# Sums of squares of the attention heads: one fp32 product with ones, or two fp32r products with ones over high and low halves

## The chip, the cores and the metric

The kernel is one program on one core of a Trainium2 chip. The metric is the time of one execution on the device in microseconds (us). Three runs of the kernel before are at hand, and one more execution was recorded by the hardware profiler.

## What is computed

Two transformer blocks over 512 tokens of width 1024. The first has two layers: a forgetting attention with 12 heads, then a retention with 12 heads, each beside 4 heads of attention over 256 memory tokens. The second block joins a long convolution with a gated linear attention (GLA) of 4 heads and a feed-forward layer. The change touches the norm of each head, in retention and in GLA:

```python
out = out.transpose(1, 0, 3, 2, 4).reshape(B, S, H, dv)      # 12 retention heads, dv = 128
out = out * lax.rsqrt(jnp.mean(out * out, axis=-1, keepdims=True) + EPS)
```

The GLA heads, also 128 wide, are normed in the same way, with a gain. All is in float32.

## The kernel before

Activations lie with features on the 128 partitions and the 512 tokens along the free dimension. A sum over the features of a head is therefore a sum over partitions, and the kernel makes it on TensorE: a product of a 128x128 matrix of ones with the squares puts the sum into every partition of a PSUM bank.

Projections are made with split operands. Each float32 operand is written as a high half in fp32r (wh, HH, OH, YH) and a low half that is the operand less its high half (wl, HL, OL, YL); a product is then three fp32r products, high by high, high by low and low by high. The copy that makes a high half runs on ACT (`copy`). Low halves of weights are made on DVE at first and on POOL (GpSimd) later, those of activations by one or the other in turn. The weights come as 294 tiles of 128x1024 by DMA on the SP queue, in a fixed plan; `split_next` makes their halves and `take` hands out the next one. `unit_f` and `unit_t` are a projection of 256 columns in two halves, 24 products of 512 columns (or 48 of 256) each; `beside` is a function that is called between the halves.

The order of the work is written out by hand. Each engine has a list (`Line`) to which the build functions append, and each engine runs its list strictly in the order of the calls. An instruction waits for the marks in its `after`.

The retention loop runs over pairs of heads, p = 0 to 5. Its calls around the change, in the kernel before and in the changed one:

```python
unit_f(HH, HL, beside=(lambda: even_norm(p - 1)) if p else None)
if p:
    ret_attend(2 * p - 1)
    keep_q()
...
rotate(p)
if p:
    ret_square(2 * p - 1)
unit_t(HH, HL, beside=(lambda: ret_rstd(2 * p - 1)) if p else None)
```

`ret_attend` puts the output of a head into bank 5 or 7. `ret_square` squares it on ACT into SQ. `ret_rstd` makes the product of ones with SQ in bank 6, and ACT makes R = exp(-0.5 ln(mean + eps)) from it, with two loads of function tables. `ret_norm` multiplies by the gate and splits the result into OH and OL, the operands of the output projection. `rotate(p)` is the rotary embedding of the next pair: SP copies QX and KX with partitions swapped, by eight small DMAs (QS, KSw), and DVE multiplies by COS and SIN and adds, ending with QR and then KR, which the scores read. The squares of an even head are called at the end of an iteration, and their product between the halves of the next one's first projection. Heads 10 and 11 are finished between the first steps of the output projection.

In GLA, `gla_square` squares a head into a temporary tile (T1 or T2; in the profile both are T), and `gla_rstd` makes the products for a pair of heads, i = 0 and then i = 1. `scales` makes row norms of the inputs with the same matrix of ones, the first time at 29 us. In the profile all instructions have line 77, that of the function that replays the lists, so that groups are told apart by their tiles.

Of the kernel before, what the change touches and what calls it, by code (L numbers as in the profile page):

```python
# [8 lines left out]
ALU = mybir.AluOpType  # L9
ACT = mybir.ActivationFunctionType  # L10
AX = mybir.AxisListType
F32 = mybir.dt.float32
F32R = mybir.dt.float32r
# [6 lines left out]
T = 512  # L20
# [157 lines left out]
def build(nc, a, out, stack):  # L178
    V, S, G, PE, SP = nc.vector, nc.scalar, nc.gpsimd, nc.tensor, nc.sync
# [7 lines left out]
    def at(name, shape, kb, dt=F32, extra=0):  # L187
        return nc.alloc_sbuf_tensor_at(name, shape, dt, offset=BASE + int(kb * KB) + extra)

    pe, dve, act, pool, sp = (Line(count("s_" + n)) for n in ("pe", "dve", "act", "pool", "sp"))  # L190
# [5 lines left out]
    s_c = [count("s_c%d" % i) for i in range(10)]  # L196
# [11 lines left out]
    OH = at("OH", [128, 16, T], 92, F32R)  # L208
    OL = at("OL", [128, 16, T], 124, F32R)
    km = [at("km0", [128, 4, 256], 108), at("km1", [128, 4, 256], 156)]  # L210
    vm = [at("vm0", [128, 2, T], 112), at("vm1", [128, 2, T], 160)]
    ident = at("ident", [128, 128], 164)
    ones = at("ones", [128, 128], 164.5)
    identb = at("identb", [128, 128], 165, BF16)
    maskb = at("maskb", [128, 128], 165.25, BF16)
    par = at("par", [128, NPAR], 165.5)
# [7 lines left out]
    eps, mod, modc = small["eps"], small["mod"], small["modc"]  # L224
# [6 lines left out]
    def copy(dst, src, after=()):  # L231
        return act.do(S.activation, dst, src, ACT.Copy, after=after)
# [4 lines left out]
    def afn(dst, src, f, after=(), **k):  # L237
        return act.do(S.activation, dst, src, f, after=after, **k)

    def tt(dst, x, y, op, after=()):  # L240
        return dve.do(V.tensor_tensor, dst, x, y, op, after=after)
# [9 lines left out]
    def vcopy(dst, src, after=()):  # L251
        return dve.do(V.tensor_copy, dst, src, after=after)

    def mm(dst, w, x, start, stop, after=(), mark=False):
        f = pe.do if mark else pe.quiet
        return f(PE.matmul, dst, w, x, start=start, stop=stop, skip_group_check=True, after=after)
# [5 lines left out]
    bank = [Bank(psum[:, i, :]) for i in range(8)]  # L262
# [199 lines left out]
    R = at("R", [128, T], C0 + 38)  # L462
# [3 lines left out]
    M = {}  # L466
    tfree = [[], []]
# [7 lines left out]
    def add_square(t, n, first, after, acc=None, scale=1.0, name="acc"):  # L475

        acc = acc or ACC
        i, q, tf = temp()
        m = afn(q[:, 0:n], t, ACT.Square, after=[*after, *tf], scale=scale)
        if first:  # L480
            m = vcopy(acc[:, 0:n], q[:, 0:n], after=[m, *M.get(name + " free", [])])
        else:
            m = tt(acc[:, 0:n], acc[:, 0:n], q[:, 0:n], ALU.add, after=[m, M[name]])
        tfree[i] = [m]
        M[name] = m
# [6 lines left out]
    def rstd(src, after, n, dim, dst, dst_free, b):  # L492

        last = M.pop("last", None)
        e = mm(b.ap[:, 0:n], ones[:, :], src, True, last is None, after=[*after, *b.free, M["cst"]], mark=True)
        if last:
            i, q, m = last
            e = mm(b.ap[:, 0:n], ones[:, :], q[:, 0:n], False, True, after=[m], mark=True)
            tfree[i] = [e]
        m = afn(dst, b.ap[:, 0:n], ACT.Ln, after=[e, M["eps"], *dst_free], scale=1.0 / dim, bias=eps[:, 0:1])  # L500
        b.free = [m]
        return e, afn(dst, dst, ACT.Exp, after=[m], scale=-0.5)
# [41 lines left out]
    for _ in range(2):  # L544
        load_raw()
    m_cst = sp.dma(SP.dma_start, ident[:, :], a["cst"][:, 0:128], s_c[0])
    m_cst = sp.dma(SP.dma_start, ones[:, :], a["cst"][:, 128:256], s_c[0])
    m_cst = sp.dma(SP.dma_start, maskf[:, :], a["cst"][:, 256:384], s_c[0])
    M["cst"], M["par"] = m_cst, m_par
    m_mem = [sp.dma(SP.dma_start, MX[:, 4 * i:4 * i + 4, :], a["memT"][:, 4 * i:4 * i + 4, :], s_mem[i])  # L550
# [3 lines left out]
    m = dve.do(V.memset, eps[:, 0:1], 1e-6)  # L554
# [13 lines left out]
    q, m, w = take_128()  # L568
# [6 lines left out]
    unit_f(HH, HL)  # L575
    for k in range(8):
        add_square(MX[:, k, :], 256, k == 0, [m_mem[k // 4]], ACC2, name="accm")
    rcol = small["tq"]

    def scales(acc, name, n, dst, c, b, b2, free=()):  # L580

        e = mm(b.ap[:, 0:n], ones[:, :], acc[:, 0:n], True, True, after=[M[name], m_cst, *b.free], mark=True)
        w = n // 128
        for t in range(w):
            e2 = mm(b2.ap[:, t:t + 1], acc[:, 128 * t:128 * t + 128], ones[:, 0:1], t == 0, t == w - 1,
                    after=[*b2.free], mark=(t == w - 1))
        M[name + " free"] = [e2]
        m = afn(dst, b.ap[:, 0:n], ACT.Ln, after=[e, M["eps"], *free], scale=1.0 / 1024, bias=eps[:, 0:1])
        m2 = afn(rcol[:, c:c + w], b2.ap[:, 0:w], ACT.Ln, after=[e2], scale=1.0 / 1024, bias=eps[:, 0:1])
        b.free, b2.free = [m], [m2]  # L590
        return afn(dst, dst, ACT.Exp, after=[m], scale=-0.5), afn(rcol[:, c:c + w], rcol[:, c:c + w], ACT.Exp, after=[m2], scale=-0.5)
# [202 lines left out]
    m = tt(CT[:, :], bank[4].ap, R[:, :], ALU.mult, after=[f_done, M["rx"]])  # L794
    bank[4].free = [m]
    m = afn(CB[:, :], CT[:, :], ACT.Abs, after=[m], bias=P("bf"))
    m2 = ts(CT[:, :], CT[:, :], P("bf"), 0.0, ALU.add, ALU.min, after=[m])
    m = afn(CB[:, :], CB[:, :], ACT.Exp, after=[m], scale=-1.0)
# [9 lines left out]
    m = afn(CB[:, :], CB[:, :], ACT.Ln, after=[m], bias=one)  # L808
    for j in range(2):
# [4 lines left out]
    m = tt(CB[:, :], CT[:, :], CB[:, :], ALU.subtract, after=[m, m2])  # L814
    m = dve.do(V.tensor_tensor_scan, CT[:, :], ones[:, 0:1].to_broadcast([128, T]), CB[:, :], 0.0, ALU.mult, ALU.add,
               after=[m])
# [23 lines left out]
    for i in range(4):  # L840
        e = tr(bank[6].ap[:, 128 * i:128 * i + 128], CT[:, 128 * i:128 * i + 128],
               after=[M["ct"], *bank[6].free], mark=(i == 3))
# [116 lines left out]
    SQ = at("SQ", [128, T], C0 + 28)  # L959
# [111 lines left out]
        M["pt readers", h % 2] = M["pt readers"] = [e]  # L1071

    def ret_square(h):
        b = bank[(5, 7)[h % 2]]
        M["sq"] = afn(SQ[:, :], b.ap, ACT.Square, after=[M["o", h], *M.get("sq free", [M["pe"]])])

    def ret_rstd(h):
        e, M["rn"] = rstd(SQ[:, :], [M["sq"]], T, 128, R[:, :], M["R free"], bank[6])
        M["sq free"] = [e]

    def ret_norm(h):
        m = M["rn"]
# [145 lines left out]
    banks = [bank[2:6], [bank[6], bank[7], bank[0], bank[1]]]  # L1228
# [4 lines left out]
    i, t, tf = temp()  # L1233
    m = tt(t[:, :], R[:, :], R[:, :], ALU.mult, after=[rm, *tf])
    m = tt(t[:, :], bank[7].ap, t[:, :], ALU.mult, after=[m, e2])
    bank[7].free, tfree[i] = [m], [m]
    R2 = at("R2", [128, T], C0 + 20)
    m = afn(R2[:, :], t[:, :], ACT.Ln, after=[m], scale=1.0 / 1024, bias=eps[:, 0:1])
    tfree[i] = [m]
    m = afn(R2[:, :], R2[:, :], ACT.Exp, after=[m], scale=-0.5)  # L1240
# [8 lines left out]
    for k in range(2):  # L1249
        e = mm(bank[4].ap[0:1, :], FT[:, k, 1, 0:1], UR[:, k, :], k == 0, k == 1, after=[*bank[4].free], mark=(k == 1))  # L1250
# [28 lines left out]
    for half in range(2):  # L1279
        o = 2 - 2 * half  # L1280
# [7 lines left out]
        for j in range(2):  # L1288
            c = 2 * half + j
            i, t, tf = temp()  # L1290
            m = conv(j, 8 + c, t[:, :], tf)
            m = tt(UT[:, c, :], t[:, :], X1[:, j, :], ALU.mult, after=[m, x1[j], en_read])
# [58 lines left out]
    banks = [[bank[6], bank[7], bank[2], bank[3]], [bank[4], bank[5], bank[6], bank[7]]]  # L1351
# [10 lines left out]
    YH, YL = at("YH", [128, 8, T], 92, F32R), at("YL", [128, 8, T], 108, F32R)  # L1362
    inverse = []
    for c in range(4):
        b = bank[4 + c]
        for odd in range(2):
            for cs in range(2):
                for ft in range(2):
                    last = odd == 1 and cs == 1 and ft == 1
                    e = mm(b.ap[:, 256 * odd:256 * odd + 256], Y[:, 4 * ft + 2 * cs + odd, 128 * c:128 * c + 128],  # L1370
                           IT[:, ft, cs, 256 * odd:256 * odd + 256], odd + cs + ft == 0, last,
                           after=[M["y", ft, 2 * cs + odd], m_it, *b.free], mark=last)
# [49 lines left out]
    q, m, w = take_128()  # L1422
# [187 lines left out]
        M["o", 0] = M["o", 1] = e  # L1610
        ss_free[:] = [e]

    def gla_square(h):
        it, t, tf = temp()
        M["gsq", h] = it, t, afn(t[:, :], bank[4 + h].ap, ACT.Square, after=[M["o", h], *tf])

    def gla_rstd(banks):
        for h in range(2):
            it, t, m = M["gsq", h]
            M["gr", h] = mm(banks[h].ap, ones[:, :], t[:, :], True, True, after=[m, *banks[h].free], mark=True)  # L1620
            tfree[it] = [M["gr", h]]
        for h in range(2):
            m = afn(RH[h][:, :], banks[h].ap, ACT.Ln, after=[M["gr", h], *rh_free[h]], scale=1.0 / 128, bias=eps[:, 0:1])
            banks[h].free = [m]
        for h in range(2):
            M["gr", h] = afn(RH[h][:, :], RH[h][:, :], ACT.Exp, after=[m], scale=-0.5)
# [23 lines left out]
    def out2(n, kh, hooks=None):  # L1650
        features(YH, YL, range(4 * kh, 4 * kh + 4), T, kh == 0, kh == 1, y_h, OUT_BANKS[n], hooks=hooks)
# [60 lines left out]
    for h in range(2):  # L1712
        for d in range(2):
            gla_within(0, d, h, False, d == 1)
        gla_square(h)
    gla_scores(1, 0, bank[0:2])
    for d in range(2):
        gla_ends(1, d)
    gla_context(1)
    gla_rstd(bank[2:4])  # L1720

    def start_second():
        gla_start(1)
# [18 lines left out]
        gla_within(1, d, h, d == 0, False)  # L1742
    gla_across(1, False)
    for h in range(2):
        gla_square(h)
    out2(1, 0, [lambda: None, lambda: gla_rstd(bank[2:4]), lambda: None, lambda: None])
    out2(2, 0)
    gla_norm(1, 0)
    gla_low(1, 0)
# [195 lines left out]
```

How the kernel before makes its waits and increments, by code:

```python
    def replay(self, eng):  # L72
        for w in self.work:
            if w[0] is None:
                eng.wait_ge(w[1], w[2])
            else:
                i = w[0](*w[1], **w[2])
                if w[3] is not None:
                    i.then_inc(w[3], w[4])
```

## Time and profile before

| | |
|---|---|
| runs | 1677.83 us median of 3 (1674.85 to 1679.32) |
| profiled execution, its own time | 1679.68 us |
| its span, first to last instruction | 1677.9 us |
| PE (TensorE) busy | 1632.9 us, 97% |
| DVE (VectorE) busy | 777.7 us, 46% |
| ACT (ScalarE) busy | 646.1 us, 39% |
| POOL (GpSimd) busy | 509.2 us, 30% |
| mean granted clock of TensorE | 0.991 of full speed |

PE is busy almost all the time. Matmuls are pipelined, so their durations overlap; the distance between the starts of two of them tells what one costs. A granted clock of 1.00 is 2.4 GHz, one of 0.50 is 1.2 GHz. An idle time in square brackets behind a row is that of its engine just before, with what ended it.

### The profile page before, as it was taken

What the parts mean: (1) busy time and instruction counts of PE and PEld (TensorE: products, weight loads), DVE (VectorE), ACT (ScalarE), POOL (GpSimd) and SP (SyncE); (2) the same over time, 40 slices, a digit from 0 to 9 for tenths busy, and PEclk for the clock granted to TensorE, in tenths of its full rate; (3) what the DMA queues carried; (4) which work ended last, traced back from release to release, by engine and by line L of the source; (5) the groups of instructions that cost most, each with busy time, mean ns of one, the idle gap of its engine ahead of it and who ended that gap; (6) DMA issues with size and microseconds to landing.
All of it is one profiled execution on the core that took longest, in us unless ns stands there. A gap on an engine that the chain in (4) does not pass through costs nothing.

```text
span 1677.9 us, 19891 instructions
## 1 busy us (share of the span) xinstructions
PE 1632.9 (97%) x8222; PEld 1333.7 (79%) x8222; DVE 777.7 (46%) x1183; ACT 646.1 (39%) x966; POOL 509.2 (30%) x245
## 2 busy tenths in 40 slices
PE   8999999999999999999999999989999899999997
PEld 7888888888878778888887767678878688888885
DVE  7877665656565344333333654752253411111113
ACT  8532333333233333444444463234434443232322
POOL 0000000000044434333333415443223355554541
PEclk9999999999999999999999999999999899999999
DMA  6454424343435223333332222122102123222321
GB/s 242 154 175 132 151 94 139 102 144 101 144 128 199 101 88 101 101 101 101 101 105 88 84 92 98 48 79 70 49 26 73 66 101 101 89 100 90 104 83 50
DMA packets 52385, 175.98 MB, mean 105 GB/s; under 512 B 6332, under 2 KB 6972, under 8 KB 51912
## 3 DMA queue, kind: packets, MB, share of 16 engines
q1 hardware_dynamic: 52296, 174.73, 30.9%
q8 instruction: 64, 1.05, 0.3%
q14 instruction: 25, 0.20, 0.0%
HBM read 169.44 MB, written 2.12 MB: 102 GB/s over the span
## 4 chain that ended last, share of the span: by engine, by line
PE 86%; DVE 8%; ACT 3%; issue 1%; POOL 1%; DMA 1%; DVEq 0%; ACTq 0%; SPq 0%
PE banks L77 86%; DVE T L77 1%; DVE TM L77 1%; ACT L77 1%; DVE ada L77 1%; DVE X L77 1%; DVE wl L77 1%; POOL wl L77 0%; DVE HL L77 0%; DVE Sc L77 0%; ACT R L77 0%; DVE Y L77 0%; ACT wh L77 0%; ACT T L77 0%; ACT Sc L77 0%
## 5 line engine op out<-in xcount | busy, mean ns | idle before, releaser
L77 POOL TENSOR_TENSOR wl<-raw,wh 128x1024 fp32r<-128x1024 f32 x173 | 426.7, 2471 | 531.5 <-ACT wh L77 531.4
L77 PE MATMUL banks<-HH,wh 128*128 128x512 f32 x1040 | 417.6, 402 | 11.7 <-ACT HH L77 11.4
L77 PE MATMUL banks<-HL,wh 128*128 128x512 f32 x1040 | 406.4, 393 | 0.8 <-DVE HL L77 0.7
L77 ACT ACTIVATE wh<-raw 128x1024 fp32r<-128x1024 f32 x246 | 258.1, 1054 | 342.5 <-PE banks L77 339.3
L77 PE MATMUL banks<-HH,wl 128*128 128x512 f32 x1040 | 286.8, 392 | 2.9 <-POOL wl L77 2.9
L77 PEld LDWEIGHTS banks<-HH,wh 128*128 128x128 f32 x1040 | 197.0, 189 | 59.4 <-ACT HH L77 13.0
L77 PEld LDWEIGHTS banks<-HL,wh 128*128 128x128 f32 x1040 | 196.9, 189 | 46.0 <-DVE HL L77 4.0
L77 PEld LDWEIGHTS banks<-HH,wl 128*128 128x128 f32 x1040 | 196.4, 189 | 45.7 <-POOL wl L77 3.7
L77 POOL TENSOR_TENSOR OL<-T,OH 128x512 fp32r<-128x512 f32 x21 | 28.1, 1340 | 505.2 <-ACT OH L77 505.2
L77 PE MATMUL banks<-wh,HH 128*128 128x256 f32 x448 | 130.5, 291 | 0.0
L77 PE MATMUL banks<-wl,HH 128*128 128x256 f32 x448 | 126.7, 283 | 0.0
L77 PE MATMUL banks<-wh,HL 128*128 128x256 f32 x448 | 126.7, 283 | 0.0
L77 DVE TENSOR_TENSOR wl<-raw,wh 128x1024 fp32r<-128x1024 f32 x73 | 87.7, 1221 | 53.1 <-ACT wh L77 52.9
L77 PE MATMUL banks<-OH,wh 128*128 128x512 f32 x256 | 103.8, 405 | 1.9 <-DVE Zt L77 1.7
L77 PE MATMUL banks<-OL,wh 128*128 128x512 f32 x256 | 99.8, 390 | 0.0
L77 PE MATMUL banks<-FHI,wh 128*128 128x512 f32 x256 | 99.6, 389 | 0.0
L77 PE MATMUL banks<-FLO,wh 128*128 128x512 f32 x256 | 99.6, 389 | 0.0
L77 DVE SCALAR_TENSOR_TENSOR X<-banks,mod,X 128x512 f32<-128x512 f32 x40 | 30.0, 751 | 147.7 <-PE banks L77 147.6
L77 PEld LDWEIGHTS banks<-wh,HH 128*128 128x128 f32 x448 | 85.9, 192 | 2.0 <-issue 1.4
L77 PEld LDWEIGHTS banks<-wh,HL 128*128 128x128 f32 x448 | 85.9, 192 | 1.5 <-issue 1.4
L77 DVE TENSOR_TENSOR T<-T 128x512 f32<-128x512 f32 x32 | 24.6, 769 | 133.2 <-ACT T L77 133.2
L77 PEld LDWEIGHTS banks<-wl,HH 128*128 128x128 f32 x448 | 85.8, 192 | 0.0
(291 smaller groups left out, 2439.2 us busy)
## 6 DMA issues: line engine op xcount, KB each, us to landing
raw<-wst_dram SPq DMA_DIRECT2D x294, 512.0 KB, 3.3
CB<-sums_dram SPq DMA_DIRECT2D x12, 256.0 KB, 3.1
D<-dec_dram SPq DMA_DIRECT2D x12, 256.0 KB, 2.8
X<-xT_dram SPq DMA_DIRECT2D x4, 512.0 KB, 5.9
out_dram<-X SPq DMA_DIRECT2D x8, 256.0 KB
QS<-QX SPq DMA_DIRECT2D x24, 64.0 KB, 2.5
KSw<-KX SPq DMA_DIRECT2D x24, 64.0 KB, 2.0
MX<-memT_dram SPq DMA_DIRECT2D x2, 512.0 KB, 9.2
```

The costliest lines, as they stand in the source:

```text
L77: i = w[0](*w[1], **w[2])
```

## The change

The matrix of ones is now an fp32r tile, `onesr`, and `ones` is the same memory read as float32. The DMA brings the values to `onesf`, and DVE casts them into `onesr` behind the squares of the memory.

`ret_square` still squares into SQ on ACT; then ACT copies SQ into OH[h], which is free until the head's result is written there, and DVE puts SQ less that into OL[h]. `ret_rstd` makes two fp32r products in one accumulation, ones by OH[h] and ones by OL[h], in place of the float32 product of ones with SQ. In GLA, `gla_square` and `gla_rstd` do the same with YH and YL. There are 12 + 4 such heads. The other products with ones stay float32.

```diff
--- before.py
+++ after.py
@@ -210,7 +210,8 @@
     km = [at("km0", [128, 4, 256], 108), at("km1", [128, 4, 256], 156)]
     vm = [at("vm0", [128, 2, T], 112), at("vm1", [128, 2, T], 160)]
     ident = at("ident", [128, 128], 164)
-    ones = at("ones", [128, 128], 164.5)
+    onesr = at("ones", [128, 128], 164.5, F32R)
+    ones = onesr[:, :].bitcast(F32)
     identb = at("identb", [128, 128], 165, BF16)
     maskb = at("maskb", [128, 128], 165.25, BF16)
     par = at("par", [128, NPAR], 165.5)
@@ -544,7 +545,8 @@
     for _ in range(2):
         load_raw()
     m_cst = sp.dma(SP.dma_start, ident[:, :], a["cst"][:, 0:128], s_c[0])
-    m_cst = sp.dma(SP.dma_start, ones[:, :], a["cst"][:, 128:256], s_c[0])
+    onesf = at("onesf", [128, 128], 184)
+    m_cst = sp.dma(SP.dma_start, onesf[:, :], a["cst"][:, 128:256], s_c[0])
     m_cst = sp.dma(SP.dma_start, maskf[:, :], a["cst"][:, 256:384], s_c[0])
     M["cst"], M["par"] = m_cst, m_par
     m_mem = [sp.dma(SP.dma_start, MX[:, 4 * i:4 * i + 4, :], a["memT"][:, 4 * i:4 * i + 4, :], s_mem[i])
@@ -575,11 +577,12 @@
     unit_f(HH, HL)
     for k in range(8):
         add_square(MX[:, k, :], 256, k == 0, [m_mem[k // 4]], ACC2, name="accm")
+    M["ones"] = vcopy(onesr[:, :], onesf[:, :], after=[m_cst])
     rcol = small["tq"]
 
     def scales(acc, name, n, dst, c, b, b2, free=()):
 
-        e = mm(b.ap[:, 0:n], ones[:, :], acc[:, 0:n], True, True, after=[M[name], m_cst, *b.free], mark=True)
+        e = mm(b.ap[:, 0:n], ones[:, :], acc[:, 0:n], True, True, after=[M[name], M["ones"], *b.free], mark=True)
         w = n // 128
         for t in range(w):
             e2 = mm(b2.ap[:, t:t + 1], acc[:, 128 * t:128 * t + 128], ones[:, 0:1], t == 0, t == w - 1,
@@ -1071,12 +1074,20 @@
         M["pt readers", h % 2] = M["pt readers"] = [e]
 
     def ret_square(h):
+
         b = bank[(5, 7)[h % 2]]
-        M["sq"] = afn(SQ[:, :], b.ap, ACT.Square, after=[M["o", h], *M.get("sq free", [M["pe"]])])
+        m = afn(SQ[:, :], b.ap, ACT.Square, after=[M["o", h], *M.get("sq free", [M["pe"]])])
+        mh = copy(OH[:, h, :], SQ[:, :], after=[m])
+        ml = tt(OL[:, h, :], SQ[:, :], OH[:, h, :].bitcast(F32), ALU.subtract, after=[mh, m])
+        M["sq free"] = M["sq"] = [ml]
 
     def ret_rstd(h):
-        e, M["rn"] = rstd(SQ[:, :], [M["sq"]], T, 128, R[:, :], M["R free"], bank[6])
-        M["sq free"] = [e]
+        b = bank[6]
+        mm(b.ap, onesr[:, :], OH[:, h, :], True, False, after=[*M["sq"], *b.free])
+        e = mm(b.ap, onesr[:, :], OL[:, h, :], False, True, mark=True)
+        m = afn(R[:, :], b.ap, ACT.Ln, after=[e, *M["R free"]], scale=1.0 / 128, bias=eps[:, 0:1])
+        b.free = [m]
+        M["rn"] = afn(R[:, :], R[:, :], ACT.Exp, after=[m], scale=-0.5)
 
     def ret_norm(h):
         m = M["rn"]
@@ -1610,15 +1621,20 @@
         M["o", 0] = M["o", 1] = e
         ss_free[:] = [e]
 
-    def gla_square(h):
+    def gla_square(i, h):
+
         it, t, tf = temp()
-        M["gsq", h] = it, t, afn(t[:, :], bank[4 + h].ap, ACT.Square, after=[M["o", h], *tf])
-
-    def gla_rstd(banks):
+        k = 4 + 2 * i + h
+        m = afn(t[:, :], bank[4 + h].ap, ACT.Square, after=[M["o", h], *tf])
+        mh = copy(YH[:, k, :], t[:, :], after=[m])
+        M["gsq", h] = tt(YL[:, k, :], t[:, :], YH[:, k, :].bitcast(F32), ALU.subtract, after=[mh, m])
+        tfree[it] = [M["gsq", h]]
+
+    def gla_rstd(i, banks):
         for h in range(2):
-            it, t, m = M["gsq", h]
-            M["gr", h] = mm(banks[h].ap, ones[:, :], t[:, :], True, True, after=[m, *banks[h].free], mark=True)
-            tfree[it] = [M["gr", h]]
+            k = 4 + 2 * i + h
+            mm(banks[h].ap, onesr[:, :], YH[:, k, :], True, False, after=[M["gsq", h], *banks[h].free])
+            M["gr", h] = mm(banks[h].ap, onesr[:, :], YL[:, k, :], False, True, mark=True)
         for h in range(2):
             m = afn(RH[h][:, :], banks[h].ap, ACT.Ln, after=[M["gr", h], *rh_free[h]], scale=1.0 / 128, bias=eps[:, 0:1])
             banks[h].free = [m]
@@ -1712,12 +1728,12 @@
     for h in range(2):
         for d in range(2):
             gla_within(0, d, h, False, d == 1)
-        gla_square(h)
+        gla_square(0, h)
     gla_scores(1, 0, bank[0:2])
     for d in range(2):
         gla_ends(1, d)
     gla_context(1)
-    gla_rstd(bank[2:4])
+    gla_rstd(0, bank[2:4])
 
     def start_second():
         gla_start(1)
@@ -1742,8 +1758,8 @@
         gla_within(1, d, h, d == 0, False)
     gla_across(1, False)
     for h in range(2):
-        gla_square(h)
-    out2(1, 0, [lambda: None, lambda: gla_rstd(bank[2:4]), lambda: None, lambda: None])
+        gla_square(1, h)
+    out2(1, 0, [lambda: None, lambda: gla_rstd(1, bank[2:4]), lambda: None, lambda: None])
     out2(2, 0)
     gla_norm(1, 0)
     gla_low(1, 0)
```

DVE, the rotation of the pair p = 1, before (QS and KSw are the swapped copies, PT and PTodd the score tiles):

```order
L77 TENSOR_TENSOR T_85<-QX,COS 128x512
L77 TENSOR_TENSOR QS<-QS,SIN 128x512
L77 TENSOR_TENSOR QR<-T_85,QS 128x512
L77 TENSOR_TENSOR T_86<-KX,COS 128x512
L77 TENSOR_TENSOR KSw<-KSw,SIN 128x512
L77 TENSOR_TENSOR KR<-T_86,KSw 128x512
L77 TENSOR_TENSOR PT<-banks,D_111 128x512
```

and after:

```order
L77 TENSOR_TENSOR T_85<-QX,COS 128x512
L77 TENSOR_TENSOR QS<-QS,SIN 128x512
L77 TENSOR_TENSOR QR<-T_85,QS 128x512
L77 TENSOR_TENSOR T_86<-KX,COS 128x512
L77 TENSOR_TENSOR KSw<-KSw,SIN 128x512
L77 TENSOR_TENSOR KR<-T_86,KSw 128x512
L77 TENSOR_TENSOR OL<-SQ,OH 128x512
L77 TENSOR_TENSOR PT<-banks,D_112 128x512
```

The subtraction for head 1 stands between KR and the first product of the scores.

PE, between the two halves of the value projection of p = 1:

```order
 L77 MATMUL banks<-wh,HL 128x256
 L77 MATMUL banks<-wl,HH 128x256
-L77 MATMUL banks<-SQ,ones 128x512
+L77 MATMUL banks<-OH,ones 128x512
+L77 MATMUL banks<-OL,ones 128x512
 L77 MATMUL banks<-wh,HH 128x256
 L77 MATMUL banks<-wh,HL 128x256
```

Two products take the place of one, between the same neighbours; the first of them now waits for DVE.

ACT, in the second pair of GLA heads:

```order
 L77 ACTIVATE YH<-T_86 128x512
 L77 ACTIVATE T_85<-banks 128x512
-L77 ACTIVATE T_86<-banks 128x512
+L77 ACTIVATE YH<-T_85 128x512
+L77 ACTIVATE T_86<-banks 128x512
+L77 ACTIVATE YH<-T_86 128x512
 L77 ACTIVATE wh<-raw 128x1024
 L77 ACT_TABLE_LOAD
```

Two copies stand ahead of the weight copy and of the table load for R.

## Rows read from the trace of the kernel before

**Rows 1.** The page, chain that ended last, share of the span by engine
```profile
PE 86%; DVE 8%; ACT 3%; issue 1%; POOL 1%; DMA 1%; DVEq 0%; ACTq 0%; SPq 0%
```

**Rows 2.** PE's waits between 660 and 900 us: us in total, times, longest
```profile
PE banks L77 <- DVE OL L77: 0.2, 1, 0.2
```

**Rows 3.** Timeline of PE: start us, us, engine line op out<-in xcount
```profile
687.71 1.02 PE L77 MATMUL banks<-SQ,ones 128*128 128x512 f32 x2
...
891.72 1.07 PE L77 MATMUL banks<-OH,wl 128*128 128x512 f32 x4
892.63 1.02 PE L77 MATMUL banks<-SQ,ones 128*128 128x512 f32 x2
893.72 0.40 PE L77 MATMUL banks<-OL,wh 128*128 128x512 f32 x1
```

**Rows 4.** Timeline of ACT and DVE beside it; ACT's group of copies
```profile
682.15 0.60 ACT L77 ACTIVATE SQ<-banks 128x512 f32<-128x512 f32 x1 [1.46 <-PE banks L77]
...
687.58 0.69 DVE L77 TENSOR_TENSOR QS<-QS,SIN 128x512 f32<-128x512 f32 x1 [4.38 <-DMA QS<-QX]
691.16 0.69 DVE L77 TENSOR_TENSOR KR<-T,KSw 128x512 f32<-128x512 f32 x1
...
L77 ACT ACTIVATE OH<-T 128x512 fp32r<-128x512 f32 x32 | 20.2, 631 | 117.1 <-DVE T L77 117.1
```

**Rows 5.** Timelines of PE and DVE, heads 3, 5, 7, 9: the product, then KR
```profile
729.85 1.02 PE L77 MATMUL banks<-SQ,ones 128*128 128x512 f32 x2
733.63 0.69 DVE L77 TENSOR_TENSOR KR<-T,KSw 128x512 f32<-128x512 f32 x1
...
771.98 1.02 PE L77 MATMUL banks<-SQ,ones 128*128 128x512 f32 x2
775.21 0.69 DVE L77 TENSOR_TENSOR KR<-T,KSw 128x512 f32<-128x512 f32 x1 [0.46 <-DVE KSw L77]
...
814.11 1.02 PE L77 MATMUL banks<-SQ,ones 128*128 128x512 f32 x2
816.69 0.69 DVE L77 TENSOR_TENSOR KR<-T,KSw 128x512 f32<-128x512 f32 x1
...
856.25 1.02 PE L77 MATMUL banks<-SQ,ones 128*128 128x512 f32 x2
859.10 0.69 DVE L77 TENSOR_TENSOR KR<-T,KSw 128x512 f32<-128x512 f32 x1
```

**Rows 6.** Stretches, granted clock third from the end; PE's waits for km, TM, HH
```profile
97.00:107.00 10.00, 7.77 (x49) 7.14 (x48) 9.21 (x9) 2.64 (x3) 1.59 (x1) 0.83 0.71 220
...
1097.00:1107.00 10.00, 5.63 (x20) 4.62 (x20) 4.21 (x7) 0.31 (x1) 8.04 (x5) 0.83 0.10 31
...
1306.00:1326.00 20.00, 14.96 (x45) 9.74 (x44) 12.13 (x17) 11.80 (x15) 4.34 (x2) 0.74 0.05 14
...
PE banks L77 <- DVE km L77: 2.2, 1, 2.2
...
PE banks L77 <- DVE TM L77: 4.4, 1, 4.4
...
PE banks L77 <- ACT HH L77: 4.4, 1, 4.4
```

**Rows 7.** Timeline of PE and DVE at the start
```profile
29.01 1.02 PE L77 MATMUL banks<-ACC,ones 128*128 128x512 f32 x2
...
29.54 0.95 DVE L77 TENSOR_TENSOR ACC<-ACC,T 128x256 f32<-128x256 f32 x2
30.86 1.23 DVE L77 TENSOR_TENSOR wl<-raw,wh 128x1024 fp32r<-128x1024 f32 x1 [0.37 <-ACT wh L77]
```

**Rows 8.** Timeline of PE and ACT in the linear-attention part
```profile
1251.60 1.09 PE L77 MATMUL banks<-VV,KE 64*128 64x256 f32 x4 [0.80 <-DVE SS L77]
...
1267.40 0.69 ACT L77 ACTIVATE R<-banks,eps 128x512 f32<-128x512 f32 x1 [0.44 <-PE banks L77]
...
1278.21 0.50 PE L77 MATMUL banks<-YL,wh 128*128 128x512 f32 x1 [0.19 <-DVE YL L77]
```

## The prediction

> **What bounds the kernel now.** I read the chain of waits first. TensorE (PE) makes up 86% of it, VectorE (DVE) 8%, ScalarE (ACT) 3% [rows 1]. So work taken off PE counts where PE is dense, and a wait put on PE counts in full unless a later wait swallows it. Next come PE's waits in the stretch where 12 of the 16 changed products stand, 660 to 900 us: one wait, 0.2 us [rows 2]. Nothing there can swallow a delay. Then the timelines of PE, ACT and DVE around one product, to see when each operand is ready and when PE asks for it [rows 3, 4], the same two moments in the other four odd heads [rows 5], what the clock did after earlier gaps of PE [rows 6], and the start and the linear-attention part, which the change touches too [rows 7, 8].
>
> **The products get cheaper.** Four fp32r products in a row take from 891.72 to 892.63, so 0.23 us each at 512 columns [rows 3]. The product of ones with SQ starts at 892.63, and the second projection product behind it at 893.72: 1.09 us, less one step of 0.23, is 0.86 us [rows 3]. Two fp32r products of the same width should take 2 x 0.23 = 0.455 us. The saving is 0.41 us a head, and for the 12 retention heads **-4.9 us**, all on PE's path. The bounds: nothing saved, if these products ran at the old rate, and 0.41.
>
> **ACT and DVE get more.** Each head adds one 128x512 copy on ACT (0.63 us [rows 4]) and one subtraction on DVE (0.69 us, the length of KR, which has the same shape [rows 4]). That is 16 x 0.63 = 10 us and 16 x 0.69 = 11 us on engines that are not the bound. What counts is whether the low half is there when PE asks for it. The same length hides or shows with its place in DVE's queue.
>
> *Even heads.* ret_square comes after the gate, and the product only after half a unit of projection. Square, copy and subtraction are 0.60 + 0.63 + 0.69 = 1.9 us; the projection between them is 24 products of 0.23, 5.5 us. Cost 0. Were the cover gone, it would be 1.3 us a head. For head 11 the same 5.5 us lie between attention and product, but ACT and DVE are busy with head 10 first; I take 0, with up to 2 us in the range for POOL's use of memory beside that subtraction.
>
> *Odd heads 1, 3, 5, 7, 9.* Here ret_square(2p-1) is written behind rotate(p). On ACT that did no harm: SQ starts at 682.15, PE asks at 687.71 [rows 3, 4]. But the new subtraction is on DVE, which runs in order, and it stands behind KR, the last step of the rotation. The rotation waits for its swap DMAs (4.38 us before QS<-QS,SIN) and KR only starts at 691.16 [rows 4]. The subtraction can start 0.60 later, as DVE's operations follow each other, lasts 0.69, and PE starts about 0.1 after it: KR's start + 1.40. PE's request comes at 687.71, so it waits 691.16 + 1.40 - 687.71 = 4.85 us. In the four later odd heads, from their two starts [rows 5]: 5.18, 4.63, 3.98, 4.25. KR's place against the request should not move, since both hang on the end of the even head's product: DVE through R, OH and the copy QX, PE through the projection products and the attention between the two requests. Sum **+22.9 us**. Bounds: 0 if KR were always early, 25 if each were like the worst. Behind the waiting product stand the second half of the value projection, the scores and all that follows on PE; ACT's Ln of R waits for it too, and the weight splits behind that Ln. They are all late by the same time, so none of them becomes a second cost. What DVE does next (the PT products) was waiting for PE anyway.
>
> *The clock.* Around these gaps of PE its granted clock went from 2.4 to 1.2 GHz for a while. Behind the wait for km (2.2 us), ten microseconds have a mean of 0.83, so (1 - 0.83) x 10 = 1.7 us of work is lost; with the wait for TM (4.4 us) it is 0.83 again, part of it inside the gap; around the wait for HH (4.4 us) it is 0.74 over 20 us, up to 5.2 us lost [rows 6]. The five new gaps are 4.0 to 5.2 us long, nearest to the two of 4.4. I take 1.6 each, the common case with a little of it inside the gap: **+8.0 us**. Bounds: 0, and 5 x 5.2 = 26.
> The Trainium skill, "TensorE: Matmul & The Clock Gate", section "HAM oscillation — how this bites in real kernels", has a kernel in which each gap costs some 1.67 us at half rate, which is 0.84 us lost. By that page's figure this term would be 5 x 0.84 = 4.2, an estimate, and the time 1702; I go by the rows, where no drop cost so little.
>
> **The start.** ones is now made by a cast on DVE that stands behind the sums of the memory squares. The first product that needs it starts at 29.01, and the last two of those sums take from 29.54 to 30.49 [rows 7]. A cast of 128 columns, a quarter of an operation that takes 0.69, is put at 0.2; PE starts at about 30.7. **+1.7 us**. DVE's next wl waits for ACT until 30.86 and is not delayed [rows 7]. Soon behind it I see no wait of PE that would give the time back. Bounds 0 and 2.2. The DMA that fetches ones keeps size and place, no other DMA moves, and POOL's order stays.
>
> **The linear-attention part.** Four products, 1.6 us less on PE. In the first pair of heads PE then waits 0.80 us for the state SS, which hangs on DVE, so its 0.8 us are swallowed [rows 8]. In the second pair ACT gets two copies, about 1.06 us, ahead of a wh copy and a table load, and the Ln of R behind these had only 0.44 us of slack [rows 8]. R comes some 0.4 to 0.6 later, and through it YL, on which PE already waits at 1278.21 [rows 8]. So the saving is hidden there as well, and the chain is longer: **+0.4 us**. Bounds -1.6 and +2.
>
> **Sum:** -4.9 + 22.9 + 8.0 + 1.7 + 0.4 = +28.1 us. The profiled execution has a span of 1677.9 us and its own time is 1679.68, so 1707.8 for it. The median of the three runs is 1677.83, 1.85 lower; against that the forecast is **1706 us**, 1.7% slower. A measurement of this kernel can tell about 0.3%, 5 us, from no change.
>
> **Rivals.**
> *The gaps come, the clock stays up* (0.10). 1706 - 8 = 1698. For it: three gaps are few to go by, and their cost differs. Against: all three had a low stretch, and the new gaps are as long or longer.
> *Long low stretches* (0.10). As after the wait for HH: if two of five lose 5.2 in place of 1.6, 1713; if all do, 1724. Against: the other two gaps lost 1.7 or less, and behind the product PE is dense here [rows 2].
> *The subtraction is in time* (0.03): the other side. KR would have to start 4.0 to 5.2 us earlier, that is, the swap DMAs of QX and KX would have to land as soon as QX and KX are there; the subtraction is late from the point where KR starts less than 1.4 us ahead of PE's request. Then only -4.9 + 1.7 + 0.4 remain: 1675, and 1672 if the linear part saves its 1.6 us and the start costs less. Against: SP issues these eight small transfers one after the other, and nothing in the change touches them.
> *The product isn't cheaper* (0.03). If ones and halves ran at the rate of the old product, a head would take 1.73 in place of 0.455: 12 x 1.27 = +15, 1721. Against: every projection product here, with weights of the same kind, takes 0.23.
>
> **How the numbers follow.** The forecast has 0.74. 1696 to 1714 takes in the case without the clock, two long low stretches, and the bounds of the small terms (-1.6 and 2); outside lie the case in time, the dear product and the upper end of the long stretches, under 0.15 together. Faster by over 0.3% 0.01, within 0.3% 0.02, slower 0.97, which is all but the case in time.
>
> **What would show it.** In the new profile OL<-SQ,OH should stand behind KR on DVE, and PE's waits should have a line for DVE OL with five of 4.0 to 5.2 us. The SQ products are gone, and OH,ones and OL,ones step by 0.23. In 660 to 900 the granted clock should fall five times. One wait for ones of 1.7 us should stand at 29 us. If PE waits for OL well under 4 us, the part on the queue is wrong; if the wait is there and the clock stays, the clock term is; if R is not later in the second pair of heads, the last term is.

## The result, and the profile after

The changed kernel takes 1710.78 us (median of 4 runs, 1709.84 to 1713.14), the kernel before in the same comparison 1677.74: 33.0 us more, a ratio of 1.0198 with a 95% interval of 1.0185 to 1.0211. The forecast was 1706, 1696 to 1714. The profiled execution has 1710.09 us, 0.7 under its median, while that of before lay 1.9 above; so the spans differ by only 30.4 us.

The page, with the span, the busy times and the chain of waits (for [rows 1]):

```profile
span 1708.3 us, 19920 instructions
...
PE 1638.0 (96%) x8222; PEld 1343.3 (79%) x8222; DVE 789.1 (46%) x1200; ACT 657.1 (38%) x982; POOL 509.1 (30%) x245
...
PE 81%; DVE 9%; ACT 5%; DMA 2%; issue 1%; SPq 1%; POOL 1%; DVEq 0%; ACTq 0%
```

PE is busy for 5 us more, part of it at half rate, and its share of the chain fell from 86% to 81%. PE's waits over the whole program, in us in total, times and longest:

```profile
PE banks L77 <- DVE OL L77: 22.3, 6, 5.1
...
PE banks L77 <- DVE ones L77: 2.3, 1, 2.3
...
PE banks L77 <- ACT YH L77: 1.0, 1, 1.0
```

None of these three lines is there before, except for one wait of 0.2 us for OL [rows 2]. Five of the six waits for OL are the new ones. DVE and PE around head 1 (for [rows 3, 4]; start us, us, engine line op, and in brackets the idle time ahead with what ended it):

```profile
691.47 0.69 DVE L77 TENSOR_TENSOR QS<-QS,SIN 128x512 f32<-128x512 f32 x1 [4.66 <-DMA QS<-QX]
...
695.04 0.69 DVE L77 TENSOR_TENSOR KR<-T,KSw 128x512 f32<-128x512 f32 x1
695.65 0.68 DVE L77 TENSOR_TENSOR OL<-SQ,OH 128x512 fp32r<-128x512 f32 x1
...
677.47 0.39 PE L77 MATMUL banks<-OH,ones 128*128 128x512 f32 x1
...
696.39 0.80 PE L77 MATMUL banks<-OH,ones 128*128 128x512 f32 x1 [4.96 <-DVE OL L77]
```

OL<-SQ,OH starts 0.61 us behind KR's start, and PE starts 0.06 us after it ends. The five rounds, by the product of an even head and the next odd one, on PE (for [rows 5]):

```profile
726.03 0.39 PE L77 MATMUL banks<-OH,ones 128*128 128x512 f32 x1
...
745.10 0.80 PE L77 MATMUL banks<-OH,ones 128*128 128x512 f32 x1 [5.11 <-DVE OL L77]
...
774.35 0.39 PE L77 MATMUL banks<-OH,ones 128*128 128x512 f32 x1
...
792.40 0.50 PE L77 MATMUL banks<-OH,ones 128*128 128x512 f32 x1 [4.09 <-DVE OL L77]
...
821.48 0.39 PE L77 MATMUL banks<-OH,ones 128*128 128x512 f32 x1
839.24 0.80 PE L77 MATMUL banks<-OH,ones 128*128 128x512 f32 x1 [3.80 <-DVE OL L77]
...
869.10 0.39 PE L77 MATMUL banks<-OH,ones 128*128 128x512 f32 x1
887.16 0.80 PE L77 MATMUL banks<-OH,ones 128*128 128x512 f32 x1 [4.09 <-DVE OL L77]
...
916.96 0.39 PE L77 MATMUL banks<-OH,ones 128*128 128x512 f32 x1
```

Before, an odd product came 14.26 us after the even one (673.45 to 687.71), and now it would come 13.85 after it, the pair being 0.41 us cheaper. It comes 18.92 after it in the first round, then 19.07, 18.05, 17.76 and 18.06. That is 22.6 us of waiting in all. From an odd product to the next even one it was 27.88 us (687.71 to 715.59), 27.47 without the 0.41, and is 29.64, 29.25, 29.08, 29.86 and 29.80: 10.3 us more in all, with the same instructions between. Why, the stretches tell (a window and its length, then busy time and count of PE, its weight loads, DVE, ACT and POOL, the granted clock, the busy share of the DMA engines and GB/s; for [rows 6]):

```profile
31.00:41.00 10.00, 9.69 (x50) 9.01 (x51) 4.42 (x7) 6.71 (x9) 0.00 (x0) 0.66 0.29 93
694.00:704.00 10.00, 7.61 (x44) 7.42 (x45) 1.99 (x3) 4.39 (x6) 2.40 (x1) 0.66 0.16 52
741.00:751.00 10.00, 5.90 (x33) 5.71 (x34) 3.84 (x6) 4.14 (x6) 0.98 (x1) 0.66 0.22 70
792.00:802.00 10.00, 9.60 (x60) 8.65 (x62) 0.89 (x2) 5.22 (x8) 2.41 (x1) 0.83 0.15 54
```

Full speed is 2.4 GHz, half is 1.2. A mean of 0.66 over 10 us is 6.8 us at 1.2 GHz; the third round, at 0.83, has 3.4. The rounds at 838 and 886 read like the first two. In windows of 1 us one sees where a stretch begins, in the first round and in the third:

```profile
694.00:695.00 1.00, 0.00 (x0) 0.00 (x0) 0.69 (x1) 0.00 (x0) 0.00 (x0) 0.62 0.90 258
...
793.00:794.00 1.00, 1.00 (x7) 1.00 (x6) 0.00 (x0) 0.81 (x2) 0.00 (x0) 0.61 0.00 0
```

In the first round the clock fell 2.2 us before PE went on at 696.39, so that much of the 6.8 us passed while PE stood still and cost nothing. In the second, fourth and fifth round it was 3.1, 1.6 and 1.5 us. In the third the clock fell 0.8 us after PE had gone on at 792.40, and all 3.4 us were paid. What was paid is 2.2, 1.8, 1.6, 2.4 and 2.3 us.

The first line of the stretches is the start, where the clock fell too. There the cast and the product that waits for it are (for [rows 7]):

```profile
31.03 0.22 DVE L77 CAST ones<-onesf 128x128 fp32r<-128x128 f32 x1
...
31.31 1.38 PE L77 MATMUL banks<-ACC,ones 128*128 128x512 f32 x2 [2.32 <-DVE ones L77]
```

Where all the time went, by places that both traces have. The second load of CB comes 4.0 us later than before (164.75 against 160.75): the start. It had been more. The product at which PE waits for km, 2.23 us in both traces, starts at 105.38 against 99.89, 5.5 us late. Behind it the kernel before had a stretch at 1.2 GHz [rows 6], and the changed one has none, which gives 1.5 us back:

```profile
102.00:112.00 10.00, 7.77 (x55) 6.71 (x54) 10.00 (x10) 3.24 (x5) 1.60 (x1) 1.00 0.63 215
```

The even product of head 0 is at 677.47 against 673.45, still 4.0. Head 10's is at 916.96 against 884.12: 28.8 us more, from the five rounds. With the saving of heads 10 and 11 it is 32.1 at the end of the heads, and 31.5 at the load of GW (1172.87 against 1141.35). Then 1.4 us come back around 1145, where the kernel before has a stretch at 1.2 GHz behind a wait for GR and the changed one has none (granted clock 0.97 against 1.00), and the linear-attention part costs 0.6.

### The profile page after: what moved, and what is told of

Read it like the earlier page. It is cut to its first block, busy times and chain, and to the rows that moved or that the text cites. A ratio compares the mean times of both kernels' runs of the same rounds, so it can differ in the third digit from the quotient of the medians.

```text
span 1708.3 us, 19920 instructions
## 1 busy us (share of the span) xinstructions
PE 1638.0 (96%) x8222; PEld 1343.3 (79%) x8222; DVE 789.1 (46%) x1200; ACT 657.1 (38%) x982; POOL 509.1 (30%) x245
## 4 chain that ended last, share of the span: by engine, by line
PE 81%; DVE 9%; ACT 5%; DMA 2%; issue 1%; SPq 1%; POOL 1%; DVEq 0%; ACTq 0%
PE banks L77 81%; DVE T L77 1%; DVE TM L77 1%; SPq L77 1%; ACT L77 1%; POOL wl L77 1%; DVE ada L77 1%; ACT wh L77 1%; DVE wl L77 1%; DVE ACC L77 1%; DVE X L77 1%; ACT R L77 1%; DMA raw<-wst_dram 1%; DMA KSw<-KX 0%; DVE Sc L77 0%
## 5 line engine op out<-in xcount | busy, mean ns | idle before, releaser
L77 PE MATMUL banks<-wh,HL 128*128 128x256 f32 x448 | 130.3, 291 | 0.0
L77 PE MATMUL banks<-wl,HH 128*128 128x256 f32 x448 | 130.2, 291 | 0.0
L77 PEld LDWEIGHTS banks<-wh,HH 128*128 128x128 f32 x448 | 90.1, 201 | 1.2 <-issue 0.2
L77 PEld LDWEIGHTS banks<-wh,HL 128*128 128x128 f32 x448 | 90.0, 201 | 0.7 <-issue 0.2
L77 PEld LDWEIGHTS banks<-wl,HH 128*128 128x128 f32 x448 | 89.6, 200 | 0.0
```

The costliest lines, as they stand in the source:

```text
L77: i = w[0](*w[1], **w[2])
```

## The experiments

The experiments ask four things: is the wait one of place in DVE's queue or of the new work as such; how much of the loss is the wait and how much the clock; do the products save what was said; and what do the cast and the linear-attention part cost. Times are medians against the kernel before, run beside.

**The subtraction ahead of the swap wait.** For the odd heads 1 to 9 it is put into rotate, between T<-QX,COS and QS<-QS,SIN; `M["low"]()` issues it there.

```diff
         m1 = tt(t[:, :], QX[:, :], COS[:, :], ALU.mult, after=[mq, M["cos"], *tf])
+        if p:
+            M["low"]()
...
+        if p:
+            ret_square(2 * p - 1, True)
         rotate(p)
-        if p:
-            ret_square(2 * p - 1)
```

> The changed kernel, with the subtraction for the odd heads 1 to 9 moved on DVE from behind KR to ahead of QS<-QS,SIN, where DVE waits some 4 us for the swap DMA; the same instructions, the same products. Theory (place in DVE's queue): the five PE waits for DVE OL go (22 us), and with them five stretches at 1.2 GHz (about 11 us lost by the spacing of the even products in the two traces): 1710.8 - 33 = 1678 us. KR starts at the same distance from PE's request as before, since the subtraction fits into the wait for the DMA. Rival (the cost is in the extra ACT copy, or in the fp32r products): PE waits or a wider step stay, and at least 10 us of the 33 remain, 1688 or more.

Measured 1678.45 us, before 1678.53, ratio 0.9996 (0.9987 to 1.0005). Its DVE and, below, PE at head 1:

```profile
683.17 2.48 DVE L77 TENSOR_TENSOR T<-QX,COS 128x512 f32<-128x512 f32 x1
685.85 0.69 DVE L77 TENSOR_TENSOR OL<-SQ,OH 128x512 fp32r<-128x512 f32 x1 [0.20 <-ACT OH L77]
690.15 0.69 DVE L77 TENSOR_TENSOR QS<-QS,SIN 128x512 f32<-128x512 f32 x1 [3.61 <-DMA QS<-QX]
...
693.71 0.69 DVE L77 TENSOR_TENSOR KR<-T,KSw 128x512 f32<-128x512 f32 x1
...
690.11 0.40 PE L77 MATMUL banks<-OH,ones 128*128 128x512 f32 x1
```

The subtraction takes part of the time in which DVE waited for the DMA, and ends 3.6 us before PE asks. PE has no wait between 660 and 890 us. Odd follows even by 13.80 us, and 32 us are gone with one instruction in another place. The copy on ACT, the subtraction and the products are the same as in the changed kernel, so none of them is what was paid for.

**The subtraction on POOL.**

```diff
+        if h % 2 and h < 11:
+            ml = pool.do(G.tensor_tensor, OL[:, h, :], SQ[:, :], OH[:, h, :].bitcast(F32), ALU.subtract, after=[mh, m])
```

> The changed kernel, with the subtraction of the odd heads 1 to 9 on POOL in place of DVE; POOL needs about 1.3 us for a 128x512 subtraction and is idle just before its wl there. Theory (DVE's queue): the waits of PE go, since POOL ends at about 684.9 in the time of the kernel before and PE asks at 687.7: 1678 us, within 2 of the run with the subtraction ahead of the swaps. Rival (the low half is late whoever makes it, because SQ or the copy is late on ACT): waits of some us stay.

Measured 1678.84 us, ratio 0.9999 (0.9989 to 1.0008). POOL and PE:

```profile
688.93 1.29 POOL L77 TENSOR_TENSOR OL<-SQ,OH 128x512 fp32r<-128x512 f32 x1 [0.79 <-ACT OH L77]
...
693.15 0.40 PE L77 MATMUL banks<-OH,ones 128*128 128x512 f32 x1
```

The slower engine, at 1.29 us for the operation, is 2.9 us early. The length of the subtraction decided nothing; what stood ahead of it did.

**The gap filled.** Sixteen products that nobody uses go ahead of the one that waits.

```diff
         b = bank[6]
+        if h % 2 and h < 11:
+            for _ in range(16):
+                mm(b.ap, onesr[:, :], HH[:, 0, :], True, True, after=[*b.free])
```

> The changed kernel with 16 more fp32r products of 512 columns (16 x 0.23 = 3.6 us) into bank 6 ahead of the product that waits, in the odd heads 1 to 9. They are work that is thrown away: the next product starts the bank anew. The low half comes when it came before, so the time until it is there is the same. Theory (the gaps cost their length and then the clock): PE's granted clock stays at 2.4 GHz there, and the kernel is faster by the clock's part, about 11 us: 1700 us. Rival (the waits alone cost the 33 us, the clock's stretch is hidden): 1711, or more by what of the 16 products doesn't fit into a gap.

Measured 1704.06 us, ratio 1.0151 (1.0137 to 1.0165): 6.7 us faster with 80 more products than the changed kernel. PE in the first round:

```profile
675.88 0.39 PE L77 MATMUL banks<-OH,ones 128*128 128x512 f32 x1
...
689.69 3.82 PE L77 MATMUL banks<-HH,ones 128*128 128x512 f32 x16
694.80 0.50 PE L77 MATMUL banks<-OH,ones 128*128 128x512 f32 x1 [1.30 <-DVE OL L77]
...
722.38 0.39 PE L77 MATMUL banks<-OH,ones 128*128 128x512 f32 x1
```

The first odd product still comes 18.92 us after the even one, exactly as without filling, but the next even one follows after 27.58 in place of 29.64. The granted clock over 660 to 920 us, first of this run, then of the changed kernel:

```profile
660.00:920.00 260.00, 253.50 (x1340) 209.09 (x1339) 91.74 (x138) 118.00 (x153) 87.52 (x40) 1.00 0.28 91
```

```profile
660.00:920.00 260.00, 237.96 (x1229) 198.39 (x1228) 90.46 (x137) 111.74 (x145) 84.58 (x39) 0.94 0.27 90
```

Over four rounds the way from the odd product to the next even one is 27.58, 27.58, 27.64 and 27.60 us; in the changed kernel these four take 7.4 us more. With the fifth, 27.60 as well, it is 9.6. So the clock's part is shown. The median moved by less than the 11 us expected because KR came later in this profile in four of the rounds, by 1.4 us in the third (19.42 us from even to odd in place of 18.05), 2.7 us in all. In the third round the first of the swap DMAs was issued 9.54 us behind the even product in both profiles, but DVE could start on QS 15.28 us behind it here and 13.73 there. Why the DMA landed later stays open.

**The old product with the new wait.**

```diff
-        mm(b.ap, onesr[:, :], OH[:, h, :], True, False, after=[*M["sq"], *b.free])
-        e = mm(b.ap, onesr[:, :], OL[:, h, :], False, True, mark=True)
+        e = mm(b.ap, ones[:, :], SQ[:, :], True, True, after=[*M["sq"], *b.free], mark=True)
+        M["sq free"] = [e]
```

> The changed kernel with the retention's two fp32r products put back to the one float32 product of ones with SQ; the copy and the subtraction are still made and the product still waits for the subtraction. Theory (fp32r pair 0.455 us, old product 0.86): 12 x 0.41 = 4.9 us more, 1715.7 us, with the same five waits. Rival (the pair saves nothing): 1710.8.

Measured 1714.73 us, ratio 1.0216 (1.0202 to 1.0230): 3.9 us above the changed kernel (3.2 if each is set against the kernel before that ran beside it), with five waits for OL of 21.9 us. The product of head 11, and the second projection product behind it, in this run:

```profile
930.07 1.02 PE L77 MATMUL banks<-SQ,ones 128*128 128x512 f32 x2
931.16 0.40 PE L77 MATMUL banks<-OL,wh 128*128 128x512 f32 x1
```

1.09 us from one to the other, as before. The same place in the changed kernel:

```profile
924.13 1.07 PE L77 MATMUL banks<-OH,wl 128*128 128x512 f32 x4
925.04 0.39 PE L77 MATMUL banks<-OH,ones 128*128 128x512 f32 x1
925.27 0.39 PE L77 MATMUL banks<-OL,ones 128*128 128x512 f32 x1
925.50 0.39 PE L77 MATMUL banks<-OH,wh 128*128 128x512 f32 x1
```

The steps are 0.23 us, and the pair takes 0.46. It is these steps that show the saving; the intervals of the medians, some 2 us either way, are wide beside it. The medians' 3.9 us are one short of 4.9; the stretches at 1.2 GHz were shorter in this profile (3.4 us in four of the five rounds), which takes time off it that has nothing to do with the product.

**The cast earlier, and the cast alone.** First the changed kernel with the cast ahead of two wl, then the kernel before with nothing but the cast.

```diff
+    M["ones"] = vcopy(onesr[:, :], onesf[:, :], after=[m_cst])
     f_done = slot_128(q, m, w, HH, HL, T, x_h, bank[4])
...
-    M["ones"] = vcopy(onesr[:, :], onesf[:, :], after=[m_cst])
     rcol = small["tq"]
```

> The changed kernel with the cast of ones moved on DVE from behind the sums of the memory squares to ahead of the two wl before them, some 6 us earlier. Theory (the start costs its 2.3 us wait and then about 1.7 us through a stretch at 1.2 GHz, since PE's landmarks are 4.0 us late from 164 us on): 1710.8 - 4.0 = 1706.8 us. Rival (the forecast's figure, the wait alone): -1.7 to -2.3, 1708.5 to 1709.1. Second rival (the time is given back at the loads of the sums): 1710.8.

Measured 1707.52 us, ratio 1.0170 (1.0157 to 1.0183), 3.3 us under the changed kernel. That lies between the 4.0 and the 2.3 that were expected by the two readings, and the medians don't tell them apart; the second load of CB comes at 161.43, 3.3 us earlier than in the changed kernel. The product and the stretch behind it:

```profile
29.71 1.02 PE L77 MATMUL banks<-ACC,ones 128*128 128x512 f32 x2
...
30.00:40.00 10.00, 10.00 (x82) 9.62 (x81) 5.61 (x8) 9.54 (x12) 0.00 (x0) 1.00 0.32 112
```

> The kernel before with one part of the change alone: ones made by the cast on DVE behind the sums of the memory squares. All products stay float32. Theory: +4.0 us, 1682 us. Rival (wait alone): +1.7 to 2.3, 1680.5.

Measured 1682.34 us, before 1677.88, ratio 1.0023 (1.0014 to 1.0031), so 4.5 us with 2.4 to 5.2 in the interval:

```profile
30.75 1.43 PE L77 MATMUL banks<-ACC,ones 128*128 128x512 f32 x2 [2.05 <-DVE ones L77]
...
30.00:40.00 10.00, 9.25 (x47) 8.52 (x47) 4.32 (x8) 7.14 (x9) 0.00 (x0) 0.66 0.24 78
```

The wait is 2.05 us here and the stretch that follows has the clock at 0.66; without the wait it is at 1.00. The second load of CB comes at 164.18, 3.4 us later than before, also without the stretch behind km. So one operation of 0.22 us on DVE costs 3 to 4 us, about half of them in the wait.

That cost is not the same in every profile. In the seven with the late cast the wait is 1.1 to 3.0 us long and the load of CB 2.4 to 5.9 us late. Where the wait was shortest, 1.3 us in the run with the subtraction ahead of the swap wait and 1.1 with the gap filled, the clock stayed up, and the load of CB was 2.8 and 2.4 us late. Part of the spread has nothing to do with the cast: from 8 us on, before the cast runs, ACT and DVE are 0.1 to 1.1 us later than in the trace of the kernel before.

**The linear-attention part as before.** gla_square and gla_rstd are those of the kernel before, the retention that of the changed one.

```diff
-        mh = copy(YH[:, k, :], t[:, :], after=[m])
-        M["gsq", h] = tt(YL[:, k, :], t[:, :], YH[:, k, :].bitcast(F32), ALU.subtract, after=[mh, m])
...
+            M["gr", h] = mm(banks[h].ap, ones[:, :], t[:, :], True, True, after=[m, *banks[h].free], mark=True)
```

> The changed kernel with the four GLA heads as before (float32 product of ones with the temporary tile). Theory (the saving of 1.6 us is hidden and ACT's copies make the chain to the output projection longer; by the two traces the part costs 0.6 us): 1710.2 us, 0.6 less. Rival (four products save their 1.6 us): 1712.4. The two differ by 2 us, and the clock's stretches can move by as much, so the landmarks in the trace decide before the medians.

Measured 1710.90 us, ratio 1.0191 (1.0177 to 1.0204). As medians this run and the changed kernel are the same, and they don't tell the two readings apart: the runs lie between 1707.95 and 1712.89. The traces tell it. From the product KEC of the second pair to the end of PE's wait for YL, first here, then in the changed kernel with ACT between:

```profile
1271.56 0.76 DVE L77 TENSOR_TENSOR KEC<-KEC,KC 128x256 f32<-128x256 f32 x2 [0.43 <-ACT KEC L77]
...
1311.44 0.50 PE L77 MATMUL banks<-YL,wh 128*128 128x512 f32 x1 [0.22 <-DVE YL L77]
```

```profile
1268.49 0.76 DVE L77 TENSOR_TENSOR KEC<-KEC,KC 128x256 f32<-128x256 f32 x2 [0.42 <-ACT KEC L77]
...
1297.08 1.28 ACT L77 ACT_TABLE_LOAD   x1
1298.38 0.69 ACT L77 ACTIVATE R<-banks,eps 128x512 f32<-128x512 f32 x1
...
1308.91 0.50 PE L77 MATMUL banks<-YL,wh 128*128 128x512 f32 x1 [0.22 <-DVE YL L77]
```

39.88 us here, 40.42 there. Before it is 39.81, and with the four heads changed it is 40.4 in the traces of both the filled gap and the early cast. The part costs 0.6 us. In the changed kernel R's Ln starts the moment the table load ends, so it is ACT, not PE, that sets it, where before ACT had 0.44 us to spare [rows 8].

**Three parts mended.** The subtraction ahead of the swap wait, the cast early, the linear-attention part as before. Retention's 12 products stay of the change, with their copies and subtractions.

> The changed kernel with three parts mended: the subtraction of the odd heads ahead of the swap wait, the cast 6 us earlier, GLA as before. What stays is 12 products at 0.41 us less. Theory: 12 x 0.41 = 4.9 us faster than the kernel before, 1673.6 us, ratio 0.997. Rival (the copies on ACT and the subtractions on DVE in the retention cost something in places other than these): 1676 or more.

Measured 1670.71 us (6 runs, 1670.55 to 1675.84), before 1677.88, ratio 0.9958 (0.9946 to 0.9970): 7.2 us faster than the kernel before. The heads, and the stretch with the wait for GR:

```profile
660.00:895.00 235.00, 234.70 (x1262) 194.94 (x1261) 94.10 (x140) 120.29 (x156) 88.19 (x41) 1.00 0.31 101
...
1135.00:1187.00 52.00, 50.05 (x369) 47.66 (x368) 10.18 (x17) 28.70 (x42) 15.61 (x7) 1.00 0.21 70
```

Nothing waits in the heads and the clock stays up. From the product of head 0 to that of head 10 it takes 206.39 us (673.50 to 879.89), before 210.67: 4.3 us for ten products, which is 0.41 each and 0.2 that I did not place. By the same reckoning the twelve give 4.9 of the 7.2 us. The second stretch, from the load of GW to KEC, gives 1.45 more (51.13 us, before 52.58), where the kernel before has a stretch at 1.2 GHz and this one has none. But of all ten traces only that of the kernel before has this stretch; the kernel before with the cast alone has none. So it may belong to that one execution, and it isn't shown that the medians' 7.2 us contain it. The remaining 0.6 us lie between head 10 and the load of GW.

## Why the prediction was right

Right in the whole and in its largest step; two terms were too small. The median lies 4.8 us above the forecast. Of these, 2.3 are in the spans (30.4 us more where 28.1 were forecast), and the rest comes from the two profiled executions, which lie 1.9 above and 0.7 below their medians.

- **The products.** Forecast -4.9 us. The pair steps by 0.23, and putting the old product back cost 3.9 or 3.2 by the medians. Right by the trace.
- **The place in DVE's queue.** Forecast 22.9 us, as 4.85, 5.18, 4.63, 3.98, 4.25. The rounds show 5.07, 5.22, 4.20, 3.91, 4.21: 22.6. The rule "KR's start + 1.40" held: 695.04 + 1.40 is 696.44, and PE started at 696.39. That KR keeps its place against PE's request held in this profile, within 0.5 us; in the run with the gap filled it came up to 1.4 us later. The upper bound, each wait like the worst, should read 5 x 5.18 = 25.9 and not 25.
- **The clock.** Forecast +8.0, 1.6 a gap; measured 10.3 from the spacing, 9.6 against the filled gap. The rows of before had a wait of 4.4 us with 1.7 lost and one with up to 5.2, and I took the first kind. Four of the five gaps had 6.8 us at 1.2 GHz, not 3.4. What was mis-sized was the length of the low stretch. That a stretch of twice the length cost only 1.8 to 2.4 us is luck for the forecast: 1.5 to 3.1 us of each passed while PE still waited, where the sum took only a little of each to lie inside the gap. The bounds, 0 and 26, held it. The figure of the Trainium skill, "TensorE: Matmul & The Clock Gate", section "HAM oscillation — how this bites in real kernels", would have made this term 4.2, an estimate; this case's traces say more than double, and the measurement decides.
- **The start.** Forecast +1.7; measured 4.0 in the two traces, and 4.5 with the cast alone, outside the bounds of 0 and 2.2 that I gave. The wait itself was near, 2.3 us: DVE ran 0.6 later in that profile from 8 us on, while PE asked at 28.99. The step that failed is that I charged the clock to the five gaps and not to this one, which was as long as the wait for km that had a low stretch before [rows 6]. The forecast also saw nothing behind the start that would give time back; the wait for km did, by 1.5 us, and without that the start would have cost 5.5. The profiles with the late cast have 2.4 to 5.9 here, so the 4.0 is one draw of several.
- **The linear-attention part.** Forecast +0.4, measured +0.6, for the reason given: the saving hidden behind ACT and DVE.
- **What lay outside the sum.** I took the stretches at 1.2 GHz elsewhere as fixed. They are not. The one behind the wait for GR vanished and gave 1.4 us back, the one behind km vanished too, though PE waited 2.23 us there in both traces, and the one behind the wait for TM has 6.8 us in place of 3.4.
- **The sum again.** With the measured terms it is -4.9 + 22.6 + 10.3 + 4.0 + 0.6 - 1.4 = +31.2 us, for spans that differ by 30.4; of the 0.8 left, 0.6 came back between the end of the heads and the load of GW.
- **Even heads and head 11.** Cost 0, as forecast: OL for head 0 starts at 673.49 and PE asks at 677.47; that for head 11 took 0.73 us beside POOL and was in time.

## What to carry to other kernels

When a product gets a new operand, read where the instruction that makes it stands in its engine's queue, and what that engine waits for ahead of it: 0.7 us of subtraction in each of five rounds cost 32 us behind a wait for a DMA, and nothing in front of it. Price a new gap of TensorE as its length and then the clock's stretch behind it, which was nearly half as much again here, and do this also for the small ones at the start. Don't take the stretches that a trace already has as fixed when the work in front of them changes. And a product that gets cheaper next to a chain on another engine gives nothing back, so change it only where TensorE is dense.

## What I had not expected of the hardware

A wait of 2.05 us at the start was followed by about 6.8 us at 1.2 GHz, as long as behind the waits of 5 us, and waits of 1.3 and 1.1 us at the same place by none. The wait for km, 2.23 us in both traces, had 3.4 us behind it before and nothing in the changed kernel. Gaps of nearly equal length had 3.4 us in one run and 6.8 in another (the round at 742 us here, and its counterpart in the run with the old product). Single runs of one kernel differ by some us, 1670.55 to 1675.84 for the mended one, with a mean granted clock of 0.993 in the fastest and 0.990 in the slowest; that it is these stretches that differ between them is likely, but only one execution of each kernel has a trace. And filling a gap with work that is thrown away made the kernel faster by 6.7 us.
